# Keys and queries of the second attention as products of 512 and 256 columns, joined by accumulating transfers

## The reference, cut to what matters

```python
n = _rmsnorm(h, norm_mix_g)
z = n @ w_in
c_a, c_g, q, k, v, qi, ki, wi, gc_logit, ga_logit = split(z)
# conformer convolution: 31 taps over the sequence, channel by channel
u = c_a * sigmoid(c_g)
u = conv31(u, conv_w) + conv_b
y_conv = silu(layernorm(u)) @ w_conv_out
# attention over the keys that an index score selects (64 of up to 256), 8 heads of 128
s = einsum('qhd,shd->hqs', q, k) * 128 ** -0.5      # where selected and causal
y_attn = (softmax(s) @ v) @ w_attn_out
h = h + (g_conv * y_conv + g_attn * y_attn) @ w_mix_out
```

## Time and profile before

| | us |
|---|---|
| median of 3 executions (918.56 to 921.36) | 920.23 |
| the profiled execution | 918.88 |
| its span, first to last instruction | 917.1 |
| PE busy | 908.4 |
| DVE busy | 680.9 |
| ACT busy | 547.9 |
| granted clock of TensorE, share of full | 0.999 |

### The profile page before, as it was taken

One profiled execution on the slowest core, in us unless ns is written; L12 is line 12 of the kernel. 1 busy time (PEld: TensorE's weight loads), 2 busy tenths in 40 slices (PEclk: granted clock), 3 DMA queues, 4 the chain that ended last, 5 costly groups with the idle time before them and its releaser, 6 DMA issues.

```text
span 917.1 us, 14020 instructions
## 1 busy us (share of the span) xinstructions
PE 908.4 (99%) x5245; PEld 785.6 (86%) x5245; DVE 680.9 (74%) x1186; ACT 547.9 (60%) x959; POOL 39.5 (4%) x47
## 2 busy tenths in 40 slices
PE   9999999999999999999999999999999999999997
PEld 7899987788888888888899997888789888888886
DVE  5879976368776666668588999998786776666666
ACT  7756767745654544456567676764945665454454
POOL 0300000000000000000012221000000000000000
PEclk9999999999999999999999999999999999999999
DMA  9955545565466556554679999656475356655551
GB/s 342 330 148 142 159 137 162 183 229 184 162 194 206 193 191 198 191 191 148 209 186 228 248 276 221 185 169 202 134 243 183 101 167 218 204 184 184 184 184 46
DMA packets 94323, 175.25 MB, mean 191 GB/s; under 512 B 8048, under 2 KB 13488, under 8 KB 94000
## 3 DMA queue, kind: packets, MB, share of 16 engines
q1 hardware_dynamic: 89568, 165.97, 56.2%
q0 software_dynamic: 4320, 7.87, 4.9%
q10 hardware_dynamic: 368, 0.52, 0.2%
HBM read 164.77 MB, written 1.05 MB: 181 GB/s over the span
## 4 chain that ended last, share of the span: by engine, by line
PE 93%; DVE 6%; issue 0%; ACT 0%; DVEq 0%; ACTq 0%
PE pb L459 90%; PE pb L463 3%; DVE YC L2120 2%; DVE wlo L1651 2%; DVE SC L2050 1%; DVE ST L2046 0%; ACT whi L1061 0%; DVE YC L2116 0%; DVE SM L1795 0%; DVE ST L1800 0%; DVE SC L2056 0%; DVE X L2397 0%; ACT QKV L1061 0%; DVE MSQ L2435 0%; DVE XS L2444 0%
## 5 line engine op out<-in xcount | busy, mean ns | idle before, releaser
L1651 DVE TENSOR_TENSOR wlo<-raw,whi 128x1024 fp32r<-128x1024 f32 (+1 forms) x298 | 353.6, 1212 | 113.6 <-ACT whi L1061 113.0
L1061 ACT ACTIVATE whi<-raw 128x1024 fp32r<-128x1024 f32 (+1 forms) x304 | 309.3, 1039 | 138.7 <-PE pb L459 117.4
L459 PE MATMUL pb<-XT,whi 128*128 128x256 f32 (+2 forms) x1456 | 312.7, 330 | 0.3 <-issue 0.2
L459 PEld LDWEIGHTS pb<-XT,whi 128*128 128x128 f32 (+1 forms) x1456 | 239.7, 190 | 20.3 <-issue 1.8
L459 PE MATMUL pb<-whi,ZO 128*128 128x512 f32 (+1 forms) x808 | 251.8, 389 | 0.0
L459 PE MATMUL pb<-XT,wlo 128*128 128x256 f32 (+1 forms) x1032 | 209.2, 282 | 0.0
L459 PEld LDWEIGHTS pb<-whi,ZO 128*128 128x128 f32 x808 | 151.3, 188 | 31.6 <-DVE wlo L1651 1.0
L459 PEld LDWEIGHTS pb<-XT,wlo 128*128 128x128 f32 (+1 forms) x1032 | 167.9, 190 | 8.7
L459 PE MATMUL pb<-whi,XT 128*128 128x512 f32 (+1 forms) x544 | 171.0, 391 | 0.0
L459 PE MATMUL pb<-wlo,ZO 128*128 128x512 f32 (+1 forms) x404 | 156.6, 388 | 0.0
L459 PEld LDWEIGHTS pb<-whi,XT 128*128 128x128 f32 x544 | 101.9, 189 | 21.0 <-issue 0.9
(11 more groups left out here) (252 smaller groups left out, 631.7 us busy)
## 6 DMA issues: line engine op xcount, KB each, us to landing
raw<-in_w_in SPq DMA_DIRECT2D x105, 512.0 KB, 4.5
raw<-in_w_ff SPq DMA_DIRECT2D x64, 512.0 KB, 5.3
raw<-in_w_up SPq DMA_DIRECT2D x32, 512.0 KB, 4.8
raw<-in_w_down SPq DMA_DIRECT2D x32, 512.0 KB, 5.8
raw<-in_w_branch_b SPq DMA_DIRECT2D x8, 512.0 KB, 5.3
raw<-in_w_out SPq DMA_DIRECT2D x8, 512.0 KB, 4.5
raw<-in_wx_kv SPq DMA_DIRECT2D x8, 512.0 KB, 5.6
YC<-PRODS POOLq DMA_DIRECT2D x16, 256.0 KB, 5.6
```

Of the source, the lines that this page charges most:

```text
L459: return e.matmul(o, l, r, start=start, stop=stop, skip_group_check=True)
L1061: return e.activation(o, i, ACT.Copy, scale=scale)
L1651: e.tensor_tensor(wlo[u % NW][:, 0:c], raw[u % NRAW][:, 0:c], whi[u % NW][:, 0:c].bitcast(F32), ALU.subtract).then_inc(lo, 1)
```

## The change

The four groups `b2_k0`, `b2_k1`, `b2_q0` and `b2_q1` are made by `cols_pair` in place of `cols`. ACT copies both halves of a bank at once (128x512): the left half to its place in `KT2` or `QT2`, the right half to a third slot, which is the memory of `V2`. The three slots are now one tensor `QKV2`. After a group's four tiles POOL issues a transfer of 512 KB that adds the group's right halves to its left ones (`join_halves`): those of `b2_k0`, `b2_k1`, `b2_q0` and `b2_q1` stand in POOL's program ahead of the transfers of taps 18, 22, 26 and 30. New waits: PE waits at the scores of head h for the joins of its key and query group (before, for ACT's copy); ACT waits before the copies of a query group for the join of the key group whose slot it overwrites, before those of `b2_k0` for DVE's last product of `b2_ca1`, and before the copies of `b2_v0` and `b2_v1` for the joins of `b2_q0` and `b2_q1`.

```diff
-HALVES = ("b1_c0", "mk", "b2_cg0", "b2_ca0")
+HALVES = ("b1_c0", "mk", "b2_cg0", "b2_ca0", "b2_k0", "b2_k1", "b2_q0", "b2_q1")
+JOINED = {"b2_k0": 0, "b2_k1": 1, "b2_q0": 2, "b2_q1": 3}
...
-        QT2 = work(W0, "QT2", 2048)[:, :].rearrange("p (h n) -> p h n", h=8)
-        KT2 = work(W0 + 2048, "KT2", 2048)[:, :].rearrange("p (h n) -> p h n", h=8)
-        V2 = work(W0 + 4096, "V2", 2048)[:, :].rearrange("p (t n) -> p t n", t=2)
+        QKV2 = work(W0, "QKV2", 6144)
+        QKR = QKV2[:, :].rearrange("p (s h n) -> p s h n", s=3, h=8)
+        QT2, KT2 = QKR[:, 0], QKR[:, 1]
+        V2 = QKV2[:, 4096:6144].rearrange("p (t n) -> p t n", t=2)
...
                     for h in {24: (0, 1), **{24 + 2 * h: (h,) for h in range(2, 8)}}.get(s, ()):
-                        e.wait_ge(*out_at[f"b2_q{h // 4}", h % 4])
+                        e.wait_ge(qk_joined[JOINED[f"b2_k{h // 4}"]], 16)
+                        e.wait_ge(qk_joined[JOINED[f"b2_q{h // 4}"]], 16)
...
-            for name in ("b2_cg1", "b2_ca1", "b2_k0", "b2_k1", "b2_q0", "b2_q1"):
+            for name in ("b2_cg1", "b2_ca1"):
                 cols(name, XT, ready, side, taps)
+            for name in JOINED:
+                cols_pair(name, XT, ready, side, taps)
...
+            def copy_halves(name):
+                d, h0 = QKR[:, 1:3] if name[3] == "k" else QKR[:, 0:3:2], 4 * int(name[4])
+                if name == "b2_k0":
+                    e.wait_ge(*out_at["b2_ca1", 3])
+                if name[3] == "q":
+                    e.wait_ge(qk_joined[JOINED[name] - 2], 16)
+                for f in range(4):
+                    e.wait_ge(*tile_at[name, f])
+                    copy(d[:, :, h0 + f, :], PB[bank_of[name, f]][:, :].rearrange("p (s n) -> p s n", s=2)).then_inc(out_a, 1)
...
-                    copy_cols(name, KT2 if name[3] == "k" else QT2, 4 * int(name[4]))
+                    copy_halves(name)
...
                 if name[3] == "v":
                     i = int(name[4])
+                    for joined in qk_joined[2:4]:
+                        e.wait_ge(joined, 16)
...
+            def join_halves(name):
+                h = 4 * int(name[4])
+                e.wait_ge(*out_at[name, 3])
+                e.dma_start(QKR[:, int(name[3] == "k"), h:h + 4, :], QKR[:, 2, h:h + 4, :],
+                            accum_op=ALU.add).then_inc(qk_joined[JOINED[name]], 16)
+
             def add_products():
                 for k in range(2, 31):
+                    for name, i in JOINED.items():
+                        if k == 18 + 4 * i:
+                            join_halves(name)
                     e.wait_ge(prod_made, k + 1)
```

More of the change, by code:

```diff
@@ L345, in build @@
         ix_done, ix_relu, ix_sum, sel_made = sem("index_scores"), sem("index_relu"), sem("index_summed"), sem("selection")
+        qk_joined = [sem(f"halves_joined_{name}") for name in JOINED]
         wi_t, wi_out, ki_moved = sem("wi_turned"), sem("wi_copied"), sem("ki_moved")
```

## The result

The changed kernel takes 927.47 us (median of 6 executions, 925.50 to 932.28) where the kernel before, in the same series, takes 919.67: 1.009 times, 95% interval 1.0074 to 1.0105. It is slower by 7.8 us. The profiled execution of the changed kernel is the slowest of its six (932.28, span 930.4), so its rows overstate the median by some 5 us, and no execution near the median was recorded with rows. It started this stretch 0.6 us later than the execution of before, from work ahead of the change.

A forecast was written before the change was run, and what follows sets the result against it. The prediction took DVE to set the pace from 513.73 to 567.3 us, with no slack in the tap stream. ACT's wait for the fourth join, +9.0 on 918.88, gave 927.9, or 929.2 as a median; range 922.0 to 935.5.

The forecast's parts named there:

- What bounds: Second layer, 513.73 to 567.3 us: DVE sets the pace although PE is busy 99% of the span.
- Products: PE's 16 units by `cols_pair`: 2.80 us each instead of 2.88, saving 1.3 of PE time, -0.2 on the path.
- heavy: Rival: late taps also stop ACT in `b2_q1`, or PE's wait brings slow products; 933.2 us, chance 0.12.
- Copies: ACT's copies of 512 columns: four take 2.1 us, +0.9 a group, hidden under ACT's idles and taken as 0.
- The stream: POOL's ring of taps: each join costs 3.0 us, three stand ahead of tap 29, moving it from 557.82 to 565.9.
- Landing: Fourth join, issued at 566.8: lands 7.0 us later, 5.5 as the last sum plus 1.5, at 573.8.
- Who waits: ACT waits for the fourth join before copying `V2`, +9.0; PE waits 6.4 at the first scores, not added.
- Sum: Whole kernel: +9.0 us on the profiled 918.88 gives 927.9, or 929.2 as a median.
- the fourth join's term: ACT's copies of `V2`, made at 564.83 before, must await the fourth join's landing at 573.8: +9.0 us.
- Hidden: Rival: the joins go through gaps between taps and nobody waits; not slower, 920.0 us, chance 0.15.
- cheap: Rival: a join costs 1.6 us as a load does, so the fourth lands at 568.2; +3.4, 923.6 us, chance 0.22.
- faster: Rival: the chain is misread, PE's 1.3 and its 1.81 of waiting are both got back; 917.1 us, chance 0.05.

The follow-up runs named there:

- less DVE work: Kernel before with 16 of DVE's tap products left out, one in each of 16 units from about 516 to 563 us: 917.53 us, ratio 0.9967.
- again: The changed kernel, unaltered, measured once more beside the other kernels on one chip: 928.51 us, 1.0085 times the kernel before.
- own room: Changed kernel with right halves in columns free until some 590 us, so ACT's V2 copies wait for no join; joins stay: 925.93 us, ratio 1.0058.
- no joins: Changed kernel without its four join transfers and every wait for them; wide products and copies stay: 921.91 us, 1.0018 times the kernel before.
- keys only: Changed kernel with pairs and joins for the two key groups alone, query groups by 256-column products: 921.22 us, 1.0006 times the kernel before.
- quarter joins: Changed kernel with joins of one head each (128 KB) at the same four places, all waits kept: 921.28 us, 1.0020 times the kernel before.
- spare sums: Kernel before plus four accumulating 512 KB transfers at the joins' places, into columns that nothing reads: 922.73 us, ratio 1.0026.

## Why the prediction was right

Forecast 929.2, measured 927.5 and 928.5. Point by point:

- **What bounds.** Right and shown: DVE sets the pace from 513 to 567 (less DVE work: faster), and PE's saving does not come through.
- **Products.** A unit by `cols_pair` takes 2.79 us (forecast 2.80). Their effect on the path was put at -0.2 with bounds 0 and -1.3. This bound failed: the kernel without joins is +1.7 in the median, as far more of its executions have the slow products. The step "it had no wait there, so nothing" did not ask what a longer wait for DVE does to the clock; the clock stood only in the heavy rival. The 7.72 against 6.13 us for 28 products show it, at a window clock of 0.79. The Trainium skill, "TensorE: Matmul & The Clock Gate", part 1, has an idle array go from 2.4 to 1.2 GHz; these traces agree: the fall stands behind a wait of 3.11 us.
- **Copies.** Four took 2.04 (forecast 2.1). Their cost was "taken as 0" under cover of ACT's idle. The cover was gone at `b2_q1`, where they stand behind a late tap 26, and PE waited 2.93 us for them. I had that stop in the heavy rival only, and for DVE's weights rather than PE's banks.
- **The stream.** 3.0 us a join: 2.95 of all engines. Tap 29 at 565.9: 566.34. Right.
- **Landing.** 7.0 us from issue: 8.7 for the join of `b2_q0` and 9.0 for the last. The step behind it, a landing time of quiet traffic with 1.5 added, was too small: with the last join under way the engines were still full (DMA share 1.01 in 568 to 576). So it landed at 575.9 instead of 573.8. That the fit cited in the prediction is one for an idle ring is my reading of it; no row shown here is of a transfer in an idle ring.
- **Who waits.** ACT for the fourth join, as forecast: it idled 7.89 us. PE at the first scores: 6.4 forecast, 3.74 seen, with the 2.93 ahead of it 6.7 in all (again: 5.89 and 0.79, also 6.7). The forecast said that 4.6 of it would remain if it ended last; own room shows 5.3, slow products included. Not adding it to the fourth join's was right too.
- **Sum.** +9.0 forecast, +7.8 measured. In the rows the fourth join's term is there and larger: ACT copies `V2` at 575.99 and, again, at 574.29, against 564.83, +11.2 and +9.5. Behind it comes a term that the sum did not have: the 28 products behind PE's third wait took 8.52 us where they took 6.13, +2.4. The two make 13.6 in the first of these executions, which took 932.28 - 918.88 = 13.4 more. So for executions like the two that have rows the forecast was 4.4 and 2.7 us short, and it fits the median because most executions lose less, in ways that no row shows. The mechanism is shown; that the number came so close is in part luck.
- **What each part is worth.** By the medians some 1.7 are PE's saving gone wrong (no joins), 3.6 more come with the joins even when ACT waits for none (own room), and 2.5 are ACT's wait for the fourth. So the term that carried the whole forecast was the last of three in a row and alone worth 2.5: the waits overlap, and the one that ends last hides the others. The forecast did not say how little would be won by removing that last one.
- **The rivals.** Hidden, cheap and faster are out. Of heavy, two parts are there (ACT stopped by a tap in `b2_q1`; half clock behind waits) in executions of 930 to 932 us.

## What to carry to other kernels

Before work is taken off the busiest engine, find out for what it waits next: earlier arrival at a wait gains nothing, and a wait that grows by a microsecond can turn slow products from something that befalls a third of the executions into the rule. So compare the clocks of all executions, and not those of one recorded execution only. A transfer added to a ring that is a pipeline itself is paid by everything behind it in that ring; put it where the pipeline has ended, and give its operands room of their own, so that no copy waits for it (room of their own was worth some 2.5 us here; of joins behind the last tap it is only shown that no one waited). And a chain of waits names the engine that ends last, not the ones that are full: look at busy time by window too before moving work there.

## What the runs showed of the hardware

- In the recorded executions PE's granted clock stayed at 1.00 behind waits of 0.79 (changed, again), 1.75 (keys only) and 1.81 us (before), and was at the lower level for some microseconds around or behind waits of 2.23 (own room), 2.93, 3.00, 3.02 (quarter joins), 3.11, 3.74 and 5.89. No boundary is to be read from this: 33 of 85 executions of the kernel before have a mean clock of 0.997 or less. I had priced the clock only for a wait of 6 us. At the lower level a product of 512 columns came every 0.43 us instead of 0.23.
- With the engines full, the time to landing grows far less than the bytes: 7.3 us for 128 KB, 5.9 to 7.2 for 256 KB, 8.9 to 10.6 for 512 KB (medians of 519 to 576, kernels with joins or spare sums; all stand in one ring, one behind the other). What goes with the bytes is what the taps behind lose.
- POOL is held 1.22 us by the issue of a join and 0.87 by that of a tap; the join's 1.22 is the same for 128 KB and for 512 KB.
